# End of the first layer: rows of experts joined on TensorE and the next norm taken tile by tile

## What is computed

```python
for l in range(DEPTH):
    ...
    hl = rmsnorm(x, norm1_w[l]) * (1 + sc1) + sh1
    hc = rmsnorm(ctx, norm1_w[l]) * (1 + csc1) + csh1
    ...
    e_idx, e_w = route_hierarchical(toks, moe_w_group[l], moe_b_group[l], moe_w_expert[l], moe_b_expert[l])
    ffn = moe_ffn(toks, e_idx, e_w, moe_w_gate[l], moe_w_up[l], moe_w_down[l])
    x = x + g2 * ffn[:n_lat].reshape(b, t, d)
    if not last:
        ctx = ctx + cg2 * ffn[n_lat:].reshape(ctx.shape)
return rmsnorm(x, final_norm_w)
```

## Time and profile before

| | us |
|---|---|
| median of three runs | 3706.56 |
| the profiled execution | 3713.84 |
| its span, first to last instruction | 3711.9 |
| end of the last product of layer 0's experts | 2039.5 |
| first product of layer 1 | 2097.13 |
| time between the two | 57.6 |

### The profile page before, as it was taken

The page is one execution under the profiler, slowest core; times in us unless marked ns, Lnnn a source line. Parts: engine busy times, 40 slices in busy tenths (PEclk is TensorE's granted clock), DMA queues, the critical chain, the costliest instruction groups (busy, mean ns, idle before and its releaser), DMA issues. The chain is left out here.

```text
span 3711.9 us, 92740 instructions
## 1 busy us (share of the span) xinstructions
PE 3456.7 (93%) x41758; PEld 1938.9 (52%) x41758; DVE 1631.2 (44%) x2896; ACT 1048.9 (28%) x1844; POOL 677.6 (18%) x583
## 2 busy tenths in 40 slices
PE   6989999999999999999999597998999999999997
PEld 3454444545666666443332345656656666774333
DVE  3584803664766663221000356824256666531111
ACT  2211002504545543111111321104145555420001
POOL 0151200302434332010000002113033333300000
PEclk8999999999999999999999799999999999999998
DMA  5103622341110111359998211833311111268996
GB/s 203 64 5 108 221 68 80 120 136 41 27 36 23 28 34 48 115 205 421 404 393 343 101 46 46 260 113 103 93 27 36 26 31 31 53 225 369 424 424 272
DMA packets 255517, 538.69 MB, mean 145 GB/s; under 512 B 49520, under 2 KB 173696, under 8 KB 222224
## 3 DMA queue, kind: packets, MB, share of 16 engines
q1 hardware_dynamic: 236064, 463.98, 34.3%
q0 software_dynamic: 19056, 68.69, 5.3%
HBM read 514.75 MB, written 17.87 MB: 143 GB/s over the span
## 5 line engine op out<-in xcount | busy, mean ns | idle before, releaser
L1299 PE MATMUL banks<-sb_h,sb_ring 128*128 128x512 f32 (+1 forms) x1344 | 476.4, 513 | 10.1 <-DMA sb_ring<-w_branch 6.5
L1816 PEld LDWEIGHTS banks<-inv 64*64 64x64 f32 x15104 | 290.3, 134 | 170.6 <-issue 168.4
L1299 PEld LDWEIGHTS banks<-sb_h,sb_ring 128*128 128x128 f32 x1344 | 255.5, 191 | 224.0 <-issue 196.6
L1816 PE MATMUL banks<-inv 64*64 64x64 f32 x15104 | 328.5, 221 | 14.3 <-issue 10.6
L1825 PE MATMUL banks<-sb_h,sb_ring 128*128 128x512 f32 (+1 forms) x672 | 329.6, 598 | 6.2 <-DMA sb_ring<-w_in 4.1
L819 PE MATMUL banks<-sb_h,sb_ring 128*128 128x512 f32 x512 | 232.1, 611 | 19.4 <-SPq L241 19.4
L3189 PE MATMUL banks<-gu,xs 128*64 128x512 f32 x768 | 169.5, 594 | 5.1 <-DMA gu<-gu_pairs 4.6
L819 PEld LDWEIGHTS banks<-sb_h,sb_ring 128*128 128x128 f32 x512 | 99.8, 197 | 138.8 <-issue 118.1
L2533 DVE COPY inv<-banks 128x512 f32<-128x512 f32 x144 | 98.9, 691 | 164.9 <-PE banks L1816 164.1
L3341 DVE TENSOR_TENSOR hrow<-hrow,banks 128x256 f32<-128x256 f32 x36 | 15.1, 421 | 355.2 <-ACT hrow L3377 355.2
L1299 PE MATMUL banks<-sb_branch,sb_ring 128*128 128x512 f32 (+1 forms) x512 | 170.9, 487 | 0.0
(11 more groups left out here) (484 smaller groups left out, 5663.8 us busy)
## 6 DMA issues: line engine op xcount, KB each, us to landing
gu<-gu_pairs SPq DMA_DIRECT2D x64, 1536.0 KB, 16.8
gu<-gu_tiles SPq DMA_DIRECT2D x57, 1024.0 KB, 8.4
sb_ring<-w_in SPq DMA_DIRECT2D x24, 2048.0 KB, 9.3
sb_ring<-gu_tiles SPq DMA_DIRECT2D x39, 1024.0 KB, 9.2
vtok<-w_mod POOLq DMA_DIRECT2D x64, 512.0 KB, 5.5
sb_ring<-down_pairs SPq DMA_DIRECT2D x32, 1024.0 KB, 14.7
sb_ring<-w_in SPq DMA_DIRECT2D x58, 512.0 KB, 3.9
sb_ring<-down_tiles SPq DMA_DIRECT2D x25, 1024.0 KB, 8.4
```

Source lines behind the costliest of these rows:

```text
L1299: mm = nc.tensor.matmul(out, left(kt), right(kt), start=kt == 0, stop=kt == KT - 1)
L1816: m = mm(k.bank[bank][H[to], at:at + w], left, right, start=start, stop=True, skip_group_check=True)
```

## The change

- The block `norm_first` goes. Its work is done at the end of `experts_rows`, by token tiles of 128, and so one barrier goes as well.
- The rows are joined by TensorE alone. While the experts run, DVE builds eight 128 by 128 diagonal matrices `diag[:, 2 * t + c]` of the shares. For each tile, `join` in TensorE's stream multiplies `first` by one and `second` by the other of them and accumulates both in PSUM, which weighs, adds and turns in one go: 16 products of 128 by 128 in place of one ACT, one DVE pass and 8 transposes.
- DVE's `join` adds the gated PSUM result to `k.x` (8 instructions of 128 by 128 for a tile). ACT squares (2 of 128 by 512), TensorE sums (8 products of 128 by 128), ACT takes `Ln` and `Exp` of 128 by 128, DVE multiplies the tile (one instruction of 128 by 8 by 128), and then ACT applies scale and shift to feature blocks 0 to 3 and DVE to 4 to 7.
- The order written on the engines is: DVE join 0, join 1, scale 0, join 2, scale 1, join 3, scale 2, scale 3; ACT squares 0, squares 1, root 0, squares 2, root 1, squares 3, root 2, root 3; TensorE join 0, join 1, sums 0, join 2, sums 1, join 3, sums 2, sums 3.
- TensorE gets eight products of two constants into bank 7, which nothing reads, between the last expert product and the first join.
- The slabs of the next layer are asked for after `got[3]` and no longer while the last rows are stored.
- The fetch of the rows waits for `dense_done`, a semaphore that DVE sets behind the leftover path, in place of `ws.used`. The leftover path runs in buffers of `experts_rows` and adds into `k.x` directly.

```diff
-def inverse_root(k, act, rinv, sums, done):
+def inverse_root(k, act, rinv, sums, done, count=1):
 
     k.nc.scalar.activation(rinv, sums, ACT.Ln, scale=1.0 / D, bias=const(k, "eps")).then_inc(done, 1)
-    act.wait_ge(done, 1)
+    act.wait_ge(done, count)
     k.nc.scalar.activation(rinv, rinv, ACT.Exp, scale=-0.5).then_inc(done, 1)
...
-def norm_first(k, flag):
-
-    nc, l = k.nc, k.layer
...
-        @block.vector
-        def _(v):
-            dense_sums(v)
-            for m in range(KT):
-                for c in range(2):
-                    x = k.x[:, m, LC * c:LC * c + LC]
-                    ins = nc.vector.scalar_tensor_tensor(x, k.acc[:, m, LC * c:LC * c + LC], k.mod[:, 40 + m, c:c + 1], x, ALU.mult, ALU.add)
-                ins.then_inc(s.updated, 1)
-            v.wait_ge(s.root, 2)
-            for m in range(KT):
-                nc.vector.tensor_tensor(k.h[:, m], k.x[:, m], rinv[:], ALU.mult).then_inc(s.normed, 1)
-
-        @block.tensor
-        def _(pe):
-            products(pe)
-            for m in range(KT):
-                pe.wait_ge(s.square, m + 1)
-                nc.tensor.matmul(sums, const(k, "ones"), sq[:, m % 3], start=m == 0, stop=m == KT - 1).then_inc(s.summed, 1)
-
-        @block.scalar
-        def _(act):
-            silus(act)
-            for m in range(KT):
-                act.wait_ge(s.updated, m + 1)
-                if m >= 3:
-                    act.wait_ge(s.summed, m - 2)
-                nc.scalar.activation(sq[:, m % 3], k.x[:, m], ACT.Square).then_inc(s.square, 1)
-            act.wait_ge(s.summed, KT)
-            inverse_root(k, act, rinv[:], sums, s.root)
-            for m in range(KT):
-                act.wait_ge(s.normed, m + 1)
-                for c in range(2):
-                    x = k.h[:, m, LC * c:LC * c + LC]
-                    nc.scalar.activation(x, x, ACT.Identity, bias=k.mod[:, m, c:c + 1], scale=k.nscale[:, 0, m, c:c + 1]).then_inc(s.affine, 1)
...
     G, ROUNDS, THIRDS = ws.groups, ws.ROUNDS, ws.THIRDS
     N = ROUNDS * P
     with ExitStack() as st:
-        s = st.enter_context(phase(nc, FRONT + " onehot turned turned_in rows_turned gu_done silu mul d_done ys_in weighed mixed back acc_in"))
+        s = st.enter_context(phase(nc, FRONT + " onehot turned turned_in rows_turned gu_done silu mul d_done ys_in diagonals dense_done"))
+        e = later_semaphores(k, DENSE + " back joined squared tail_sum tail_root scaled affine")
 
         def sb(name, *shape):
             return st.enter_context(nc.sbuf_tensor(f"{name}{l}", [P, *shape], F32))
 
         row, xs, hrow, hid = sb("xrow", 2, D), sb("xs", 2, KT, N), sb("hrow", ROUNDS, HID), sb("hid", HT, N)
         spare = k.acc[:].rearrange("p a c -> p (a c)")
-        ys, oh = (spare[:, a:a + b * c].rearrange("p (b c) -> p b c", c=c) for a, b, c in ((0, ROUNDS, 512), (512 * ROUNDS, NT, P)))
+        ys, oh, diag = (spare[:, a:a + b * c].rearrange("p (b c) -> p b c", c=c)
...
+        held, wide_x = ws.gu[:].rearrange("p j e c -> p (j e c)"), xs[:].rearrange("p j kt c -> p (j kt c)")
+        at = [sum(DENSE_ROOM[1:i]) for i in range(1, 5)]
+        room = [wide_x] + [held[:, at[i]:at[i + 1]] for i in range(3)] + [row[:, 0, 0:TT]]
+        sq_tail = wide_x[:, 0:2 * D].rearrange("p (j f c) -> p j f c", j=2, f=KT)
+        rinv = hrow[:, 0, 0:2 * P].rearrange("p (j c) -> p j c", j=2)
+        tail_sums = k.bank[4:6]
+
+        def token_tile(a, t, half=None):
+            return a[:, slice(0, KT) if half is None else slice(4 * half, 4 * half + 4), P * t:P * t + P]
+
+        def joined(t, half):
+            return k.bank[2 * (t % 2) + half]
+
+        def add_out(m, out):
+            for c in range(2):
+                x = k.x[:, m, LC * c:LC * c + LC]
+                ins = nc.vector.scalar_tensor_tensor(x, out[:, LC * c:LC * c + LC], k.mod[:, 40 + m, c:c + 1], x, ALU.mult, ALU.add)
+            return ins
+
+        weights, dense_products, silus, dense_sums = experts_dense(k, room, e, l, rt.flag, 0, add_out)
 
         def third(g, n):
             return THIRDS * g + n
...
-            ask_next_slabs(k, sp, [(ws.used, ws.total - 2), (ws.used, ws.total)])
             sp.wait_ge(s.stored, 16)
+            sp.wait_ge(ws.used, ws.total)
+            weights(sp)
+            for t in range(NT - 1):
+                sp.wait_ge(got[t], 32)
+            ask_next_slabs(k, sp, [(got[NT - 1], 32), (got[NT - 1], 32)])
 
         @block.gpsimd
         def _(pool):
@@ -3323,7 +3311,7 @@
             put_rows(G - 1, 1)
             for i in range(ROUNDS):
                 pool.wait_ge(stored[i], 16 * 2 * G)
-            pool.wait_ge(ws.used, ws.total)
+            pool.wait_ge(s.dense_done, 1)
             for t in range(NT):
                 for c, buf in enumerate((first, second)):
                     nc.gpsimd.indirect_dma_start(buf[:, t], None, k.d.rows_out, index(t, c), bounds_check=EXPERTS * C - 1, oob_is_err=False)\
...
                         normed(v, m - 1)
+                    elif m == KT + 1:
+                        for t in range(NT):
+                            for c in range(2):
+                                ins = nc.vector.tensor_scalar(diag[:, 2 * t + c], const(k, "ident"), rt.share[:, t, c:c + 1], None, ALU.mult)
+                        ins.then_inc(s.diagonals, 1)
+            dense_sums(v)
+            v.sem_inc(s.dense_done, 1)
+
+            def join(t):
+                for half in range(2):
+                    v.wait_ge(e.back, 2 * t + half + 1)
+                    for f in range(4):
+                        m = 4 * half + f
+                        x = k.x[:, m, P * t:P * t + P]
+                        ins = nc.vector.scalar_tensor_tensor(x, joined(t, half)[:, P * f:P * f + P], k.mod[:, 40 + m, P * t // LC:P * t // LC + 1], x,
+                                                             ALU.mult, ALU.add)
+                    ins.then_inc(e.joined, 1)
+
+            def scale(t):
+                v.wait_ge(e.tail_root, 2 * t + 2)
+                h, c = token_tile(k.h, t), P * t // LC
+                nc.vector.tensor_tensor(h, token_tile(k.x, t), rinv[:, t % 2].unsqueeze(1).to_broadcast([P, KT, P]), ALU.mult).then_inc(e.scaled, 1)
+                v.wait_ge(e.scaled, t + 1)
+                for m in range(4, KT):
+                    ins = nc.vector.tensor_scalar(h[:, m], h[:, m], k.nscale[:, 0, m, c:c + 1], k.mod[:, m, c:c + 1], ALU.mult, ALU.add)
+
             for t in range(NT):
-                v.wait_ge(s.weighed, t + 1)
-                nc.vector.scalar_tensor_tensor(first[:, t], second[:, t], rt.share[:, t, 1:2], first[:, t], ALU.mult, ALU.add).then_inc(s.mixed, 1)
+                join(t)
+                if t:
+                    scale(t - 1)
+            scale(NT - 1)
 
         @block.scalar
         def _(act):
             take_hidden(2)
             take_out(G - 1, 0)
             take_out(G - 1, 1)
-            act.wait_ge(s.last, 1)
+            silus(act)
+            nc.scalar.preload_act_table_set("natural_log")
+
+            def squares_of(t):
+                if t >= 2:
+                    act.wait_ge(e.tail_sum, t - 1)
+                for half in range(2):
+                    act.wait_ge(e.joined, 2 * t + half + 1)
+                    ac(sq_tail[:, t % 2, 4 * half:4 * half + 4], token_tile(k.x, t, half), ACT.Square).then_inc(e.squared, 1)
+
+            def root_and_affine(t):
+                act.wait_ge(e.tail_sum, t + 1)
+                if t >= 2:
+                    act.wait_ge(e.scaled, t - 1)
+                inverse_root(k, act, rinv[:, t % 2], tail_sums[t % 2][:, 0:P], e.tail_root, 2 * t + 1)
+                act.wait_ge(e.scaled, t + 1)
+                h, c = token_tile(k.h, t), P * t // LC
+                for m in range(4):
+                    ac(h[:, m], h[:, m], ACT.Identity, bias=k.mod[:, m, c:c + 1], scale=k.nscale[:, 0, m, c:c + 1]).then_inc(e.affine, 1)
+
             for t in range(NT):
-                act.wait_ge(got[t], 32)
-                ac(first[:, t], first[:, t], ACT.Copy, scale=rt.share[:, t, 0:1]).then_inc(s.weighed, 1)
+                squares_of(t)
                 if t:
-                    take_back(t - 1)
-            take_back(NT - 1)
+                    root_and_affine(t - 1)
+            root_and_affine(NT - 1)
 
         @block.tensor
         def _(pe):
+                mm(k.bank[7], const(k, "ident"), const(k, "scan"), start=True, stop=True)
+
+            def join(t):
+                pe.wait_ge(got[t], 32)
                 for half in range(2):
                     if t >= 2:
-                        pe.wait_ge(s.acc_in, 2 * (t - 2) + half + 1)
+                        pe.wait_ge(e.joined, 2 * (t - 2) + half + 1)
                     for f in range(4):
-                        m = turn(k.bank[2 * (t % 2) + half][:, P * f:P * f + P], first[:, t, 512 * half + P * f:512 * half + P * f + P], ident)
-                    m.then_inc(s.back, 1)
```

(38 more changed lines are left out.)

40 lines of the change are left out of this document (18 added, 22 removed).

## The result

The changed kernel took 3715.58 us (median of 20 runs, 3707.81 to 3723.92), the kernel before 3708.69 (20 runs, 3702.25 to 3716.69): ratio 1.0019 [1.0012, 1.0025]. It is 0.19% slower, some 7 us, where I had forecast 7 us faster. The difference is within the 0.3% that I called no change, but the time lies above my range.

A forecast was written before the change was run, and what follows sets the result against it. One chain between the layers, 57.6 us without TensorE work, was taken to bound the kernel. Earlier fetches, joins, turns and root steps ended the block at 2088.7 against 2095.65; 7 us off the 3706.56 median gave 3699.6, range 3690 to 3709.

The forecast's parts named there:

- no time of their own: Unread products before the first join: 7.3 us from 2041.5 to 2048.8, ahead of the first rows, so adding nothing.
- one set: Rival on ACT's tables: all seven loads go, gain 16 us, 3690.6 us; chance 0.02.
- Stores and fetches: After the last expert product: last store lands in 2.3 us instead of 7.5, first fetch near 2043.75, 5.1 us earlier.
- stores land no earlier: Rival on the last stores: slabs were not what held them, costing 5.1 us of the gain, 3704.7 us; chance 0.12.
- Slabs: Next layer's weights: asked for at 2059.3, in by 2070, needed only at 2090, so hidden by some 20 us.
- TensorE after the flag: Start of the unread products behind the last expert product: flag costs 1.25 us, so they start near 2041.5.
- Clock at the joins: TensorE's joins: taken at 2.4 GHz, 0.124 us a matmul, 3.95 us a join.
- My rival of the low clock: TensorE stays at 1.2 GHz: joins 7.9 us, end 6.9 us later than before, 3713.4 us; chance 0.04.
- Turns: ACT and DVE chain from one root to the next while joins are left: 8.8 us each, hand-overs 0.2.
- Root 3's step: Last root, no join ahead: multiply, ACT's four scale-and-shifts, loads, `Ln`, `Exp` and hand-overs, 5.85 us, to 2086.15.
- The drain: ACT's table switches: skill's rule of about 1380 ns beside each load, estimated 9.7 us for seven; refused, trace shows none.
- `Ln` and `Exp` need no change of tables: Rival on ACT's norm chain: all seven table loads go, gain 16 us, 3690.6 us; chance 0.02.

The follow-up runs named there:

- the padded version: The changed kernel with 48 unread small products (192 TensorE instructions) added behind its last sums; 3708.16 us, ratio 0.9984 to the kernel before.
- The bare version: The changed kernel with one table set, without the eight unread products, 48 small ones behind the last sums; 3693.63 us, ratio 0.9938 to the kernel before.

## Why the prediction was wrong

The failed step stands in the prediction's first paragraph: "a microsecond off the 57.6 between is a microsecond off the program". I took the stage's 7 us off the median of the whole program and put the rest of it at nothing. "A change of time elsewhere in the program" is named only as what would make me wrong, without a price or a chance. The change's 320 more instructions on TensorE moved its fetches in layer 1 by 64, and rwkv_heads there pays 12 to 14 us. With that shift made whole the change has a ratio of 0.9984, that is 5.9 us faster (2.6 to 9.3).

That comes close to the 7 us of the forecast partly by luck, for the stage gave half of them: 3.7 us in the first profile, 4.2 in the padded version's. The second step that failed is in the sum, the unread products with "no time of their own" (below).

Of the 13.8 us, the records show 6.7 as more idleness, nearly all `issue`, and 7.1 as longer products. That the longer products follow from the stalls by way of the clock is an inference; that both go with the shift is shown. Also, the range of 3690 to 3709 doesn't leave out "one set", as I wrote: its 3690.6 lies inside.

Within the stage, forecast 50.7 us, measured 53.9:

- *Stores and fetches: right.* 2.6 us to land for 2.3; first fetch 4.9 us behind the last expert product, from 9.4, forecast 4.3. The rival "stores land no earlier" fell, and the early slabs brought the old landing back. Yet join 0 waited for TensorE and not for its rows, with late slabs and with early ones.
- *Slabs: right.* Asked for at 2060.95, nobody waits for them.
- *TensorE after the flag: wrong, and the largest error of the stage.* I took 1.25 us for the flag, from a block's start on DVE. With the flag and the branch over the unrolled loop of the leftover path TensorE was idle for 5.89 us, without them for 0.72. So the unread products began at half clock, took 9.27 us for 7.3, and ended 3.3 us after the rows were due, where I had them 2 us ahead. "No time of their own" became 3.2 us: join 0 starts at 2055.67, its rows were due at 2052.4. Root 0 came 2.9 us later than my sum allows (2066.8; my 2062.7 is 23.2 us behind the last expert product, here 2063.9).
- *Clock at the joins: right* in the change (0.11 us a matmul, first join 3.6 us), for a wrong reason: the products warmed TensorE by being late. Where they came in time, without the leftover path, TensorE stood idle for 3.2 us behind them and the clock had fallen again by the first join. My rival of the low clock had its price too high. The bare version began its joins at half clock and was no slower: joins 2 and 3 lie beside the turns, and the granted clock was back at 1.00 from 2056 on, 5 us into the joins, where the rival kept it low to the end.
- *Turns: right within 0.4.* 8.44 for 8.8: the join in DVE is 2.15 for 2.4, and the hand-overs come to 0.1 for 0.2. Root 3's step is 6.24 for 5.85, since ACT's four take 1.65, not 1.3; the last 2.9 for 2.55; the step to layer 1 1.7 for 1.48. These together add 0.3 us; the other 2.9 of the missing 3.2 are root 0's: join 0 started 3.7 us later than forecast (3.2 by TensorE, 0.5 by the first fetch), and the shorter joins gave 0.8 back.
- *The drain: rightly refused.* Taking the seven loads away shortened the stage by 9.0 to 9.4 us, where 7 x 1.28 is 9.0. The Trainium skill, ScalarE: Activation LUTs, section What ACT_TABLE_LOAD costs, says about 1380 ns more for each; the trace disagrees.
- *"`Ln` and `Exp` need no change of tables": rightly refused for this kernel, wrongly as a fact of the chip.* The Trainium skill, ScalarE: Activation LUTs, section Table sets: the hidden batching unit, says that one set holds both, and the run with one table set agrees: none of the seven loads is left. With "natural_log" named the program got seven, and the kernel before, with none named in its norm, two. I read a choice of the program as if it were the chip's, and passed by 9 us.

## What to carry to other kernels

A change that adds or removes instructions on an engine that is busy all the time moves the fetch points of everything behind it. Count its instructions, look for `issue` waits that end just behind an instruction packet in the code that follows, and compare lengths block by block before believing a total. A difference of a few tenths of a per cent is tested by padding: if a whole fetch (here 256 instructions) brings the old time back and half of one doesn't, it was placement, and the change is to be judged at equal placement. A block's length from one profile needs the same care: set the profiled execution beside the median of its runs before reading a few microseconds out of it. And work put in "while TensorE is idle" needs its start read from that engine's own records; with a taken branch over a long loop it began 5.9 us late here.

## What the runs showed of the hardware

- TensorE's instructions arrive as DMA packets of 16 KB in queue q8, one for 251 recorded matmuls and weight loads in rwkv_heads. If the period is the 256 instructions that the pads point to, that is 64 bytes each. Such a packet was 6.8 us apart from the one before it during a burst at 103.5% DMA share, and TensorE stood for 3.71 us.
- The place of the code within a fetch moved that block by 10 to 20 us: 650 to 654 us at shifts of 0, 192 and 256, 661 to 671 at 64 and 128.
- Flag and branch that skip the leftover path on TensorE: 5.89 us of idleness with one instruction packet in it and one just behind it, 8.52 with slabs on the queues, 0.72 without flag, branch and path.
- Without the leftover path TensorE's granted clock fell to 0.50 by the end of 3.2 us of idleness, so eight products that ended 3.2 us early didn't keep it up for the joins.
